# A hybrid trunk step on eight cores: first loads in another order, normalisation steps reordered, the convolution's coefficient blocks built ahead, merge tiles moved into the convolution

## The chip, the cores and the metric

One Trainium2 chip, all 8 of its cores. Each core computes one prompt sequence of 2048 positions and 64 sample rows (16 sequences of 4 positions) with the full weights; the cores do not talk to each other. The metric is the device time in microseconds (us) of the slowest core for one launch.

## What is computed

One layer of a decoder trunk. `xn` is the RMS-normalised input; `pa, pb, pg` are column blocks of one projection.

```python
proj = xn @ w_in                      # 1024 -> 6*1024
a_val, a_gate = split(pa)
glu = a_val * sigmoid(a_gate)
ca  = causal_depthwise_conv(concat(conv_prev, glu), w=(31, 1024)) + b
y_a = silu(layernorm(ca)) @ w_a_out
u, v = split(gelu(pb))
v_n = layernorm(v)                    # mixed over chunks of 128 positions by W_s (8 heads)
y_b = (u * (tril(W_s) @ v_n + b_s)) @ w_b_out
out = (sigmoid(g_a) * y_a + sigmoid(g_b) * y_b) @ w_out
h   = h + out
# channel mixer
a, b = split(rmsnorm(h) @ w_up)       # 1024 -> 2*2816
h   = h + (gelu(causal_depthwise_conv(a, 3)) * b) @ w_down
y   = rmsnorm(h)
```

Outputs are y for prompt and sample, the last rows of the convolutions' inputs, and the normalised v rows of the sample.

## The kernel before

The kernel keeps everything in one SBUF array, `arena`, cut by byte offsets into named views, and one PSUM array of 8 banks that `rbank()` hands out in turn. Helpers (`mm`, `tr`, `act`, `tt`, `tsc`, `stt`, `cp`, `mset`, lines 303 to 337) record one instruction each into the list of its engine, and `Sched` adds the semaphore waits by the bytes touched. So each engine runs its list strictly in the order in which the Python code is written; nothing reorders it. DMAs issued by `S.dma("sp", ...)` stand in SyncE's list, and those of `S.dma("pool", ...)`, which all weight loads use (`load_unit`, 128x1024 f32 in memory, bf16 in SBUF), stand in GpSimd's list between its arithmetic. A DMA also waits for the one before it on its stream (`s_g0` to `s_g23` for SyncE, `s_q0` to `s_q15` for GpSimd).

The stages, in order of the program:

1. **u**: 17 slabs of x (128 rows, the last of 64) are loaded (`xload`), squared and summed on ScalarE (`sq`), scaled on VectorE (`xscale`), turned by 8 TensorE transposes (`xtr`) and copied out as `xnT` (`norm_evac`, VectorE). `xstep` runs these as a software pipeline: step i squares slab i, scales i-1, transposes and copies i-2. `u_mm(c0, w, j)` multiplies w columns by weight block j (8 matmuls) and applies GELU on ScalarE. There are 8 x buffers (`NXB`), and `xscale(c)` also issues `xload(c + 8)` into the buffer that it has read.
2. **v**: for each chunk c `v_mm` (16 matmuls of 512 columns, two GELUs), `v_stats` (two bn_stats, aggregate, add on VectorE, power -0.5 on GpSimd, then a scalar_tensor_tensor that centres), `v_scale` on ScalarE, and `v_mix` (10 matmuls, then two tensor_tensor on VectorE), which runs two chunks behind.
3. **GLU**: two column halves `cb`, each with `s_glu(cb)` for the sample (64 matmuls of 96 columns) and 16 steps p of 16 matmuls with 512 columns, a tanh on ScalarE and one VectorE operation; VectorE also does 8 operations of the sample's convolution in each step (`s_conv`). In the second half `x_trans` transposes groups of channels for the convolution.
4. **convolution**: the depthwise convolution of the prompt is done on TensorE in 16 blocks, `conv(i)`, with 24 matmuls of 128 columns each, against a block of coefficients that `t_build(i)` spreads out from `coef`, in 8 parts: 4 on GpSimd, 3 on ScalarE, 1 on VectorE. Three slots hold such blocks (`tb_t`). Results go to `Y`, whose row q takes 4096 bytes; blocks 0 to 7 write the upper half of each row and blocks 8 to 15 the lower half.
5. **q and merge**: layer norm of Y (`q_stats`, `q_z`), transposes (`q_tr`) and, between them, `run_fill(1)`, which takes one merge tile `half_b(j, ti)` (16 matmuls) from a list of 10; then the rest of the merge.
6. **w_out** with the second RMS norm (`wo_mm`, `n2_scale`, `n2_tr`), **FFN up** (22 blocks of 10 tile halves) and **down** (34 units of 22 matmuls, then the last norm and the store).

## Time and profile before

| | |
|---|---|
| times of three executions | 1183.58, 1340.87 (median), 1375.21 us |
| the profiled execution | 1183.48 us; its slowest core spans 1181.8 us (all cores 1175.4 to 1181.8) |
| TensorE busy | 1088.8 us (92%) |
| VectorE, ScalarE, GpSimd busy | 627.6, 441.2, 186.4 us |
| granted TensorE clock, mean | 0.98 |

The span runs from the first to the last instruction of the slowest core. An engine's busy time counts its compute instructions; "idle before" is the time it stood still just before an instruction, with what released it. The granted clock is 1.00 at 2.4 GHz and 0.5 at 1.2 GHz.

### The profile page before, as it was taken

To read this page: it belongs to the slowest core of one execution; us is meant where nothing else is said; L and a number is where in the kernel's file an instruction comes from. 1 tells how busy PE (TensorE), PEld (TensorE's weight loads), DVE (VectorE), ACT (ScalarE), POOL (GpSimd) and SP (SyncE) were. 2 spreads that over 40 slices of the span, in tenths; PEclk is the share of its full clock that TensorE was granted. 3 is DMA by queue.
4 is the path that set the end of the run, shared out by engine and by line. 5 is a ranking of instruction groups with operands and counts; after the bars stand their busy time and mean duration, and the time that the engine had idled before them with its cause. 6 is when DMAs were issued, how large, how long until landed. Compare 5 with 4: busy or idle time off the path is not lost.

```text
span 1181.8 us, 18831 instructions; the slowest of 8 cores (1175.4 to 1181.8 us)
## 1 busy us (share of the span) xinstructions
PE 1088.8 (92%) x6439; PEld 611.5 (52%) x6527; DVE 627.6 (53%) x1246; ACT 441.2 (37%) x795; POOL 186.4 (16%) x389
## 2 busy tenths in 40 slices
PE   2789986999976999999999999999999999799997
PEld 1546443767664655555554445555555555344443
DVE  1443778565688923333345656666666666223322
ACT  2343433112482731111115555555555555011111
POOL 2323011000175300010001111111111111000000
PEclk9999998999998999999999999999999999899999
DMA  9557201402013032224247742333333322422331
GB/s 241 148 90 118 44 1 18 93 2 41 1 29 55 1 54 37 39 36 82 41 82 248 246 118 45 55 54 55 54 54 55 54 45 43 113 108 107 109 121 73
DMA packets 36140, 88.86 MB, mean 75 GB/s; under 512 B 4112, under 2 KB 6288, under 8 KB 36048
## 3 DMA queue, kind: packets, MB, share of 16 engines
q0 software_dynamic: 21552, 38.75, 20.2%
q1 hardware_dynamic: 14496, 48.92, 12.7%
q8 instruction: 53, 0.87, 0.3%
q14 instruction: 39, 0.32, 0.1%
HBM read 108.05 MB, written 20.04 MB: 108 GB/s over the span
## 4 chain that ended last, share of the span: by engine, by line
PE 80%; DVE 6%; issue 4%; ACT 4%; DMA 4%; POOL 2%; DVEq 0%; SPq 0%; POOLq 0%; ACTq 0%
PE ps L303 78%; ACT arena L314 2%; DMA arena<-w_all 2%; PE ps L306 2%; DVE arena L317 2%; DVE arena L327 2%; DVE arena L575 2%; ACT arena L311 1%; POOL arena L317 1%; DMA arena<-x_p 1%; DVE arena L322 0%; DMA o_vs<-arena 0%; DVE arena L578 0%; DVEq L194 0%; DVE arena L324 0%
## 5 line engine op out<-in xcount | busy, mean ns | idle before, releaser
L303 PE MATMUL ps<-arena 128*128 128x512 bf16 (+7 forms) x5895 | 1060.0, 339 | 63.8 <-DMA arena<-w_all 20.0
L303 PEld LDWEIGHTS ps<-arena 128*128 128x128 bf16 (+1 forms) x5983 | 579.1, 103 | 528.0 <-issue 89.8
L314 ACT ACTIVATE arena<-ps 128x512 f32<-128x512 f32 (+6 forms) x348 | 177.7, 523 | 350.8 <-PE ps L303 263.4
L327 DVE SCALAR_TENSOR_TENSOR arena<-arena 128x64 f32<-128x64 bf16 (+5 forms) x539 | 247.1, 493 | 47.7 <-POOL arena L317 27.1
L314 ACT ACTIVATE arena<-arena 128x512 f32<-128x512 f32 (+4 forms) x192 | 125.9, 676 | 198.1 <-DVE arena L327 178.5
L327 DVE SCALAR_TENSOR_TENSOR arena<-arena,ps 128x512 f32<-128x512 f32 (+4 forms) x120 | 70.0, 589 | 174.4 <-PE ps L303 164.4
L317 DVE TENSOR_TENSOR arena<-arena,ps 128x512 bf16<-128x512 f32 (+2 forms) x143 | 86.4, 614 | 84.9 <-ACT arena L314 84.9
L317 POOL TENSOR_TENSOR arena<-arena 128x1 f32<-128x1 f32 (+1 forms) x85 | 54.6, 647 | 412.6 <-DVE arena L324 290.7
L311 ACT ACTIVATE arena<-arena 128x1024 bf16<-128x1024 f32 (+1 forms) x51 | 53.8, 1054 | 172.4 <-DVE arena L317 149.6
L317 DVE TENSOR_TENSOR arena<-ps,arena 128x1024 bf16<-128x1024 bf16 (+4 forms) x72 | 65.4, 908 | 88.6 <-PE ps L303 86.4
L180 POOL DMA_DIRECT2D arena<-w_all x138 | 74.1, 547 | 195.6 <-PE ps L303 180.0
L314 ACT ACTIVATE arena<-ps,arena 128x512 f32<-128x512 f32 (+3 forms) x150 | 101.2, 705 | 4.1 <-PE ps L306 4.1
L324 DVE TENSOR_SCALAR arena<-arena 128x1 f32<-128x1 f32 (+4 forms) x80 | 23.6, 314 | 109.1 <-ACT arena L311 99.3
L306 PE MATMUL ps<-arena 128*128 128x128 bf16 (+2 forms) x544 | 41.5, 223 | 21.6 <-DVE arena L322 15.1
L334 POOL COPY arena<-arena 128x32 f32<-128x32 f32 (+1 forms) x66 | 13.9, 212 | 260.0 <-ACT arena L314 257.1
L306 PEld LDWEIGHTS ps<-arena 128*128 128x128 bf16 (+2 forms) x544 | 34.4, 100 | 34.3 <-issue 29.3
L327 DVE SCALAR_TENSOR_TENSOR arena<-ps,arena 128x512 f32<-128x512 f32 (+1 forms) x66 | 43.5, 681 | 11.3 <-PE ps L303 11.1
L324 POOL TENSOR_SCALAR arena<-arena 128x384 bf16<-128x384 bf16 x64 | 36.6, 586 | 0.2
L575 DVE BATCH_NORM_STATS2 arena<-arena 128x6 f32<-128x512 f32 (+1 forms) x34 | 23.5, 690 | 18.7 <-ACT arena L314 17.1
L322 DVE TENSOR_SCALAR arena<-arena 128x1 f32<-128x1 f32 (+4 forms) x67 | 29.8, 444 | 3.6
L317 DVE TENSOR_TENSOR arena<-arena 128x512 bf16<-128x512 f32 (+4 forms) x45 | 26.4, 586 | 4.6 <-DVE arena L317 0.2
L337 POOL MEMSET arena<- 128x32 bf16 (+5 forms) x23 | 4.0, 178 | 120.4 <-ACT arena L314 120.4
(19 smaller groups left out, 51.5 us busy)
## 6 DMA issues: line engine op xcount, KB each, us to landing
arena<-w_all POOLq DMA_DIRECT2D x138, 256.0 KB, 5.0
arena<-x_p SPq DMA_DIRECT2D x32, 512.0 KB, 5.1
h1s<-arena SPq DMA_DIRECT2D x16, 512.0 KB, 3.2
arena<-h1s SPq DMA_DIRECT2D x16, 512.0 KB, 3.9
o_yp<-arena SPq DMA_DIRECT2D x16, 512.0 KB, 2.9
o_ch<-st_a SPq DMA_DIRECT2D x1, 1664.0 KB, 18.7
arena<-dw_t POOLq DMA_DIRECT2D x4, 384.0 KB, 4.5
arena<-st_a POOLq DMA_DIRECT2D x1, 960.0 KB, 18.5
```

The lines of the kernel that those rows point to most:

```text
L180: e.items.append(("op", lambda q, o=out, i=in_: q.dma_start(out=o, in_=i), stream, 16))
L303: S.op("pe", lambda q: q.matmul(out, lhsT=lhsT, rhs=rhs, start=start, stop=stop), [out], [lhsT, rhs], inc=stop)
L306: S.op("pe", lambda q: q.transpose(out=out, in_=in_, identity=ident), [out], [in_, ident], inc=inc)
L311: S.op("act", lambda q: q.activation(out=out, in_=in_, func=func, scale=scale, bias=bias, accum_out=accum), [out, accum], ins)
L314: S.op("act", lambda q: q.activation(out=out, in_=in_, func=func, scale=scale, bias=bias), [out], ins)
L317: S.op(en, lambda q: q.tensor_tensor(out=out, in0=in0, in1=in1, op=op), [out], [in0, in1])
L322: S.op(en, lambda q: q.tensor_scalar(out=out, in0=in0, scalar1=s1, scalar2=None, op0=op0), [out], ins)
L324: S.op(en, lambda q: q.tensor_scalar(out=out, in0=in0, scalar1=s1, scalar2=s2, op0=op0, op1=op1), [out], ins)
L327: S.op("dve", lambda q: q.scalar_tensor_tensor(out=out, in0=in0, scalar=scalar, in1=in1, op0=op0, op1=op1), [out], [in0, in1] + ([scalar] ...
L334: S.op(en, lambda q: q.tensor_copy(out=out, in_=in_), [out], [in_])
L337: S.op("pool", lambda q: q.memset(out, v), [out], [])
L575: S.op("dve", lambda q, i=i, a=a: q.bn_stats(out=s[:cs, 6 * i:6 * i + 6], in_=a), [s[:cs, 6 * i:6 * i + 6]], [a])
```

## The change

- **u stage.** Four x slabs instead of eight are issued at once, with two weight blocks beside them; weight blocks 2 and 3 and then 4 to 7 are issued from GpSimd between the first four normalisations. The slabs 4 to 7 are issued after that, each behind the landing of a weight block. A first GELU on one column is issued before any data. The first eight groups of 128 columns are computed in tiles of 256 columns, and a table `at` says after which tile which `xstep` comes.
- **v stage.** The centring is taken out of `v_stats` as `v_center` and put behind the mix of the chunk two before. The last scale and mixes are interleaved with `s_glu(1)`, which is cut in two parts.
- **Convolution.** `t_build` takes a string of engines for its 8 parts and has another layout; six slots instead of three, the three new ones in the lower halves of rows of Y, so that blocks 0, 1, 3, 4 and 5 are built on GpSimd in the second GLU half, block 2 after it, and 6 to 15 in the convolution. Four weight blocks of the merge are loaded in the convolution (at block 5), and four merge tiles run in it (after blocks 9, 11, 13 and 15); the list has 15 tiles. The state for the sample's convolution is loaded ahead of the GLU weights. `q_stats` adds and takes the power for four rows in one instruction.
- **w_out.** The transposes run two chunks behind instead of one, with three buffers.
- **Down.** The first four units run their first 20 matmuls before any runs the last two. The last chunk is normalised and stored in two halves.

```diff
+        for c in range(1, 4):
             xload(c)
+        mset(nh, -0.5)
+        act(stat[0][:, 31:32], nh, AF.Gelu)
...
+        for c in range(4):
+            sq(c)
+            if c:
+                norm_evac(c - 1, 34)
+            if 0 < c < 3:
+                u_load()
+            xscale(c)
+            xtr(c)
+            if c == 2:
+                u_mm(0, 256, 0)
+            if c == 3:
+                u_mm(0, 256, 1)
         u_load()
+        norm_evac(3, 34)
+        nready[0] = 4
+        for c in range(4, 8):
+            xload(c, after=[wtok[min(c - 2, len(wtok) - 1)]])
+            if len(uW) < 8:
+                u_load()
+        work = [(0, 256, j) for j in (2, 3)] + [(256, 256, j) for j in range(4)]
+        work += [(c0, 256, j) for j in range(4, 8) for c0 in (0, 256)]
+        work += [(c0, 256, j) for c0 in (512, 768) for j in range(8)]
+        work += [(c0, w, j) for c0, w in TILES[2:] for j in range(8)]
+        at = {2: 4, 5: 5, 8: 6, 11: 7, 15: 8, 18: 9, 21: 10, 24: 11, 27: 12, 29: 13, 31: 14, 33: 15, 35: 16, 37: 17, 39: 18}
         for n, (c0, w, j) in enumerate(work):
+            while nready[0] < -(-(c0 + w) // 128) and nready[0] < 17:
+                xstep()
             u_mm(c0, w, j)
+            if n in at and nstep[0] <= at[n]:
+                xstep()
...
-            if i < len(order):
-                v_stats(order[i])
+            v_stats(order[i])
             if i >= 2:
                 v_mix(order[i - 2])
+            v_center(order[i])
...
+        tslots = [tslot(R1, 2048), tslot(R1 + 6144, 2048), tslot(R2, 2048),
+                  tslot(OFF_D + 4 * 4096, 4096), tslot(OFF_D + 12 * 4096, 4096), tslot(OFF_D + 7 * 4096, 16384)]
+        tb_of = lambda i: tslots[i] if i < 6 else tslots[i % 3]
...
+        v_scale(order[16])
+        s_glu(1, (0,))
+        v_mix(order[15])
         for cb in (1, 0):
-            s_glu(cb)
+            if cb == 1:
+                s_glu(1, (1,))
+                v_mix(order[16])
+            else:
+                s_glu(0)
...
-                    if p in (2, 4):
-                        coef_load((p - 2) // 2)
-                    if p in (10, 12):
-                        t_build((p - 10) // 2)
+                    if p in (0, 1):
+                        coef_load(p)
+                    if p in (3, 5, 8, 10, 13):
+                        t_build({3: 0, 5: 1, 8: 3, 10: 4, 13: 5}[p], "pppppppp")
...
+        t_build(2, "daadaapp")
+        for i in range(16):
+            if i + 8 < 16:
+                x_trans(i + 8)
+            conv(i)
+            if i < 3:
+                t_build(i + 6, "pppppaaa")
+            elif 6 <= i < 13:
+                t_build(i + 3, "ppppaaaa")
+            if i in (1, 2):
+                coef_load(i + 1)
...
+            if i == 5:
+                mload(4)
...
+            if i in (9, 11, 13, 15):
+                run_fill(1)
...
-            if i >= 1:
-                n2_tr(i - 1)
+            if i >= 2:
+                n2_tr(i - 2)
             n2_scale(i)
...
+        early = [(i, q, rbank()) for i in range(2) for q in range(2)]
+        for i, q, b in early:
+            dn_mm(i, q, b, range(20))
+        for i, q, b in early:
+            dn_mm(i, q, b, range(20, NFF))
+            dn_add(i, q, b)
```

SyncE's list at the start of the program, before. `x_p` is the input x, a row is one slab, `x7` means seven such rows, `s_act` and `s_dve` are ScalarE's and VectorE's counters.

```order
L180 DMA arena<-x_p 128x1024
L180 DMA arena<-col_a 128x288
L180 DMA arena<-x_p 128x1024 x7
L180 DMA arena<-x_p 128x1024 [waits s_g0,s_act,s_dve]
L180 DMA arena<-x_p 128x1024 [waits s_dve] x7
```

The same place after the change.

```order
L180 DMA arena<-x_p 128x1024
L180 DMA arena<-col_a 128x288
L180 DMA arena<-x_p 128x1024 x3
L180 DMA arena<-x_p 128x1024 [waits s_g0,s_act,s_dve]
L180 DMA arena<-x_p 128x1024 [waits s_g2,s_act,s_dve]
L180 DMA arena<-x_p 128x1024 [waits s_g3,s_act,s_dve]
L180 DMA arena<-x_p 128x1024 [waits s_g4,s_act,s_dve]
L180 DMA arena<-x_p 128x1024 [waits s_q2]
L180 DMA arena<-x_p 128x1024 [waits s_q3]
L180 DMA arena<-x_p 128x1024 [waits s_q4]
L180 DMA arena<-x_p 128x1024 [waits s_q5]
```

The slabs 8 to 11, issued by `xscale(0)` to `xscale(3)` in the new first loop (the rows that wait for `s_g0`, `s_g2`, `s_g3`, `s_g4`), now stand ahead of the slabs 4 to 7, which wait for the landing of the weight blocks 2 to 5 (`s_q2` to `s_q5`).

VectorE's list in the v stage, one chunk of 16 alike, before.

```order
L575 BN_STATS arena<-arena 128x6 [waits s_act]
L575 BN_STATS arena<-arena 128x6 [waits s_act,s_dve]
L578 BN_AGGR arena<-arena 128x2 [waits s_dve]
L322 TENSOR_SCALAR arena<-arena 128x1 [waits s_dve]
L327 SCALAR_TENSOR_TENSOR arena<-arena 128x1024 [waits s_pool]
L317 TENSOR_TENSOR arena<-arena,ps 128x4x128 [waits s_pe] x2
```

The same place after the change.

```order
L588 BN_STATS arena<-arena 128x6 [waits s_act]
L588 BN_STATS arena<-arena 128x6 [waits s_act,s_dve]
L591 BN_AGGR arena<-arena 128x2 [waits s_dve]
L322 TENSOR_SCALAR arena<-arena 128x1 [waits s_dve]
L317 TENSOR_TENSOR arena<-arena,ps 128x4x128 [waits s_pe] x2
L327 SCALAR_TENSOR_TENSOR arena<-arena 128x1024 [waits s_pool]
```

The centring, which waits for GpSimd's power, and the two products of the mix have changed places.

GpSimd's list in the convolution after the change, from its part of block 6 to its part of block 9. The 128x3x128 rows are parts of `t_build`, the MEMSETs belong to `x_trans` and wait for its copy on ScalarE, `dw_t` is the source of `coef`.

```order
L324 TENSOR_SCALAR arena<-arena 128x3x128 [waits s_pool,s_pe]
L324 TENSOR_SCALAR arena<-arena 128x3x128 x4
L337 MEMSET arena 128x8x4 [waits s_act]
L324 TENSOR_SCALAR arena<-arena 128x3x128 [waits s_pool,s_pe]
L324 TENSOR_SCALAR arena<-arena 128x3x128 x4
L180 DMA arena<-dw_t 128x1536 [waits s_pool,s_dve]
L337 MEMSET arena 128x8x4 [waits s_act]
L324 TENSOR_SCALAR arena<-arena 128x3x128 [waits s_q5,s_pe]
L324 TENSOR_SCALAR arena<-arena 128x3x128 x4
L180 DMA arena<-dw_t 128x1536 [waits s_pool]
L337 MEMSET arena 128x8x4 [waits s_act] x3
L180 DMA arena<-w_all 128x1024 x4
```

Before, the third coefficient load stood four blocks ahead of its first reader; now its first reader (the row that waits for `s_q5`) is the next arithmetic behind it.

## Rows read from the trace of the kernel before

**Rows 1.** Busy time by stretch, whole core; the second line names the columns.

```profile
core 2 of [0, 1, 2, 3, 4, 5, 6, 7], span 1181.8 us
core 2: us, PE busy (x) PEld busy (x) DVE busy (x) ACT busy (x) POOL busy (x), PEclk, DMA share, GB/s
0.00:115.60 115.60, 81.67 (x542) 51.14 (x548) 39.85 (x65) 41.96 (x85) 36.37 (x62) 0.96 0.68 149
115.60:211.60 96.00, 79.52 (x480) 40.38 (x489) 71.41 (x121) 36.28 (x51) 10.26 (x18) 0.93 0.19 33
211.60:329.20 117.60, 116.17 (x628) 79.47 (x640) 73.60 (x290) 30.97 (x49) 6.77 (x17) 1.00 0.14 27
329.20:373.30 44.10, 28.39 (x456) 26.22 (x458) 40.47 (x67) 30.34 (x53) 36.70 (x73) 0.98 0.19 30
373.30:414.80 41.50, 39.05 (x293) 23.60 (x296) 32.45 (x77) 24.49 (x38) 12.52 (x20) 0.94 0.19 31
414.80:618.80 204.00, 203.12 (x1187) 112.92 (x1201) 67.32 (x121) 41.85 (x84) 17.49 (x33) 1.00 0.30 52
```

**Rows 2.** DMA queues of the page: packets, MB, share of 16 engines.

```profile
q0 software_dynamic: 21552, 38.75, 20.2%
q1 hardware_dynamic: 14496, 48.92, 12.7%
```

**Rows 3.** Timeline, u stage: start, length, instruction, idle before and its releaser.

```profile
10.49 1.06 ACT L311 ACTIVATE arena<-arena 128x1024 bf16<-128x1024 f32 x1 [2.52 <-DMA arena<-x_p]
...
14.58 0.58 POOL L180 DMA_DIRECT2D arena<-w_all  x1
...
23.66 1.87 PE L303 MATMUL ps<-arena 128*128 128x256 bf16 x8 [4.07 <-DMA arena<-w_all]
...
55.28 5.32 PE L303 MATMUL ps<-arena 128*128 128x512 bf16 x12 [4.10 <-DVE arena L317]
...
61.73 3.62 PE L303 MATMUL ps<-arena 128*128 128x512 bf16 x16
65.19 0.61 PE L306 MATMUL ps<-arena 128*128 128x128 bf16 x8
```

**Rows 4.** Timeline, end of the v stage, VectorE and TensorE.

```profile
192.24 1.28 DVE L327 SCALAR_TENSOR_TENSOR arena<-arena 128x1024 f32<-128x1024 f32 x1 [0.80 <-POOL arena L317]
...
194.64 1.48 DVE L575 BATCH_NORM_STATS2 arena<-arena 128x6 f32<-128x512 f32 x2
...
199.89 1.49 DVE L575 BATCH_NORM_STATS2 arena<-arena 128x6 f32<-128x512 f32 x2
...
205.42 10.75 PE L303 MATMUL ps<-arena 128*128 128x128 bf16 x93 [3.39 <-ACT arena L314]
```

**Rows 5.** Timeline, second GLU half, VectorE without and with GpSimd building.

```profile
299.34 1.65 DVE L327 SCALAR_TENSOR_TENSOR arena<-arena 128x64 f32<-128x64 bf16 x8
...
314.07 1.90 DVE L327 SCALAR_TENSOR_TENSOR arena<-arena 128x64 f32<-128x64 bf16 x8
```

**Rows 6.** Groups by form, 330 to 374 us: busy us, mean ns, idle before.

```profile
L324 POOL TENSOR_SCALAR arena<-arena 128x384 bf16<-128x384 bf16 x56 | 31.7, 581 | 0.2
L303 PE MATMUL ps<-arena 128*128 128x128 bf16 x384 | 24.0, 219 | 9.6 <-ACT arena L314 4.5 <-DVE arena L322 3.1 <-DVE arena L327 1.6
```

**Rows 7.** Timeline, first merge tiles, TensorE.

```profile
373.30 12.79 PE L303 MATMUL ps<-arena 128*128 128x512 bf16 x47 [6.14 <-DMA arena<-w_all]
```

**Rows 8.** DMA issues of the page: count, KB each, us to landing.

```profile
arena<-dw_t POOLq DMA_DIRECT2D x4, 384.0 KB, 4.5
```

**Rows 9.** Waits of TensorE, 615 to 702 us: us in total, times, longest.

```profile
PE ps L306 <- ACT arena L314: 4.6, 9, 0.8
```

**Rows 10.** Timeline, start of the down stage, TensorE.

```profile
1011.97 0.61 PE L303 MATMUL ps<-arena 128*64 128x512 bf16 x1 [5.81 <-DMA arena<-w_all]
1014.27 7.96 PE L303 MATMUL ps<-arena 128*64 128x512 bf16 x23 [1.70 <-DMA arena<-w_all]
```

**Rows 11.** Timeline, the last chunk.

```profile
1175.17 1.06 ACT L311 ACTIVATE arena<-arena 128x1024 bf16<-128x1024 f32 x1 [8.35 <-DVE arena L317]
```

More of the change, by code:

```diff
@@ L413, in build_program @@
         S.dma("sp", colA, col_a)
-        for c in range(1, NXB):
+        for c in range(1, 4):
             xload(c)
+        mset(nh, -0.5)
+        act(stat[0][:, 31:32], nh, AF.Gelu)
         mset(ident_f, 0.0)
@@ L619, in build_program @@
         order = [16] + list(range(16))
-        for i in range(len(order) + 2):
-            if i < len(order):
-                v_mm(order[i])
-            if 1 <= i <= len(order):
+        for i in range(len(order)):
+            v_mm(order[i])
+            if i >= 1:
                 v_scale(order[i - 1])
-            if i < len(order):
-                v_stats(order[i])
+            v_stats(order[i])
             if i >= 2:
                 v_mix(order[i - 2])
+            v_center(order[i])
         sg = [view(R2 + 2048 * i, F32, (128, 512)) for i in range(3)]
@@ L671, in build_program, with s_glu @@
         s_conv = []
-        def s_glu(cb):
-            for jp in range(2):
+        def s_glu(cb, parts=(0, 1)):
+            for jp in parts:
                 b = rbank()
@@ L688, in s_glu @@
                 cp("dve", glub[:, j0:j0 + 2, 480:544], gluS[:, j0:j0 + 2, 32:96])
-            for k in range(CW):
+            for k in range(CW) if 1 in parts else ():
                 for j in range(cb * 4, cb * 4 + 4):
@@ L696, in s_glu @@
                                                            yS[:, j, :], ALU.mult, ALU.add))
-            if cb == 0:
+            if cb == 0 and 1 in parts:
                 S.dma("sp", o_ca, gluS)
@@ L792, in mload, with run_fill @@
                 key = morder[mnext[0]]
-                wtile[key] = load_unit(mkind[key], RING[mnext[0] % 6])
+                wtile[key] = load_unit(mkind[key], OFF_C + 25344 + 2048 * mnext[0] if mnext[0] < 4 else RING[(mnext[0] - 4) % 6])
                 mnext[0] += 1
-        mload(6)
         scount = [0]
+        late = [False]
+        fill = [(j, ti) for j in range(3) for ti in range(5)]
+        def run_fill(n):
+            for _ in range(n):
+                if fill:
+                    half_b(*fill.pop(0))
         xqn = lambda a, nn: a.rearrange("p (q n) -> p n q", n=nn)
@@ L916, in build_program @@
         h1 = [view(OFF_C + 12288 + 4096 * i, F32, (128, D)) for i in range(3)]
-        xs2 = [view(OFF_D + 2048 * i, BF16, (128, D)) for i in range(2)]
+        xs2 = [view(OFF_D + 2048 * i, BF16, (128, D)) for i in range(3)]
+        UPR = [RING[i] for i in (2, 3, 0, 1, 4, 5)]
         upW = {}
```

215 lines of the change are left out of this document (115 added, 100 removed).

## The prediction

> **What bounds the kernel now.** I read the table by stretch first [rows 1], to see where TensorE (PE) isn't working. Between 414.8 and 618.8 us it is busy 203.12 of 204.00 us at a granted clock of 1.00, and in the GLU stage 116.17 of 117.60: nothing is to be had there. The losses lie where dependence chains or loads set the pace. The u stage takes 115.6 us with 81.67 busy and a clock of 0.96, the v stage 96.0 with 79.52 busy at 0.93, the convolution 44.1 with 28.39 busy. The stretch behind it has 39.05 of 41.5 busy, but at 0.94. So the idle time is one loss and the half clock behind it is another: after 4.10 us of idle, 12 matmuls of 512 columns take 5.32 us (443 ns each), against 3.46 us for 16 a little later (65.19 less 61.73, 216 ns each) [rows 3]. The clock was at its lower level, 1.2 GHz, for those 12. I then read, stretch by stretch, which wait ends last.
>
> **The u stage.** At 10.49 us the second slab of x has landed, but weight block 1 is issued only at 14.58, behind GpSimd's powers and behind eight slabs in the DMA engines, and TensorE has waited 4.07 us for it when it starts at 23.66 [rows 3]. One transfer is priced by the queues: q0 moved 38.75 MB in 20.2% of 1181.8 us, so 0.262 MB of a weight block is 1.6 us of all engines; a 0.524 MB slab on q1 is 12.7% × 1181.8 / 48.92 × 0.524 = 1.6 us too [rows 2]. After the change block 1 is issued at about 3 us and blocks 2 and 3 from about 13.5, (slab 1's landing, 1.25 us of square, the power and the issue), so the first tiles of 256 columns run from about 18 us on. Against this stands SyncE's new order: slabs 8 to 11 go ahead of 4 to 7, though they are needed last. By 20 us some 11 transfers are through; four slabs and four weight blocks alternate, slab 4 lands at about 28 to 29 and slab 7 near 36. `sq(4)` stands in ScalarE's list from tile n=2 on and holds up the GELUs behind it. Slab 5 lands near 32; its square, the VectorE steps behind it and the transposes of slab 4 (which stand behind tile n=8) put those at about 34.4, and the copy of slab 5, on which tile n=14 waits, ends near 41.5. Before, the same point (first 512 columns done, next ones ready) is 55.28. From it to 115.6 is 60.3 us; the idle at its start is left out of that already, and the 12 slow matmuls cost 12 × (443 − 216) = 2.7 us, so 57.6 remain. This would end the stage at 99.1. I add 1.5 for a half clock after the waits at n=9 and n=14: 100.6. **Saving 15 us.** Bounds: 0 (slabs 4 to 7 land as late as the stage can bear, and the warm-up is paid twice), and 22 (they don't bind).
>
> **The v stage.** VectorE sets the pace: from one chunk's bn_stats to the next is 199.89 − 194.64 = 5.25 us, of which 0.80 is idle before the centring, waiting for the power on GpSimd [rows 4]. With the mix's products in this gap the period is 4.45. The products are ready: their matmuls stand behind `v_mm` of the same step, as the second GELU does. TensorE's own work per chunk is 16 + 2 matmuls of 512 columns at 216 ns and 8 of a quarter of that, 4.3 us, just under it. 15 steady steps × 0.80 = 12.0. At the end TensorE waits 3.39 us for the last scale [rows 4], then does the last mix and `s_glu(1)` behind a cold start. With the two halves of `s_glu(1)` in the gap I take 4. **Saving 16 us.** Bounds: 8 (TensorE's 4.3 is 4.6 in truth, and half of the end) and 17. The GpSimd list now has the sample's state load in front of 16 weight loads, and the last of those waits for its stream; v's first power is behind them. That may cost 0 to 4 of this, and I take none, as the loads are issued some 18 us ahead.
>
> **GLU.** TensorE sets it, nothing gained. GpSimd gets 40 parts of `t_build` here instead of 8. With 4 parts beside it, a group of 8 VectorE operations of `s_conv` takes 1.90 us instead of 1.65 [rows 5], so 40 parts add 10 × 0.25 = 2.5 us to an engine that is busy 73.60 of 117.6 [rows 1]. Cost 0; if that cover were gone, 2.5.
> The Trainium skill (SBUF — State Buffer, Who interferes with whom) says that a VectorE instruction with two SBUF inputs and a GpSimd instruction that reads SBUF exclude each other for a whole instruction. By that, 40 builds at 581 ns would put 23 us on VectorE here, and the stage would end some 7 us later; rows 5 show a quarter of a microsecond for four.
>
> **Convolution and q.** Before, TensorE is idle 9.6 us in it, waiting for ScalarE's and VectorE's parts, then 6.14 for the first merge weights, and 12 cold matmuls open the merge (47 in 12.79 us) [rows 6, 7]. Now four merge tiles (three of 16 × 216 ns and one of 288 columns, 1.95 us: 12.3) go into it and blocks 0 to 5 are ready. But GpSimd becomes the pace. It has 15 parts for blocks 6 to 8 and 28 for 9 to 15, 43 × 0.581 = 25.0 us [rows 6]; the part of block 8 waits for a coefficient load just issued, 4.5 us [rows 8], with ScalarE's part of it and the copies of `x_trans` behind it; four weight loads cost 4 × 0.58 more to issue (the row of 14.58 us in [rows 3]). On a time line from the stage's start: block 6 can begin on GpSimd at about 5.3, when ScalarE has done its parts of block 2 and the first copy of `x_trans`; blocks 6 and 7 take 5 × 0.581 each and end at 11.2; the issue of the load (0.6) and its 4.5 us give 16.3, block 8's five parts 19.2, the second coefficient load and the four weight loads 22.0, block 9's four parts 24.4. TensorE then has 7 blocks of 24 × 58 ns = 1.4 us and 12.3 us of tiles left, and ends at about 46.5 against 44.1 before, with the four tiles done. Later blocks need 2.3 us each on GpSimd, less than a block and half a tile on TensorE, 3.1. That gains 12.3 − 2.4 = 9.9; the cold start of the merge (12 × 0.22 = 2.6) goes too, and the batched power about 0.5. **Saving 13 us.** Bounds: 3 (GpSimd's parts at a stride cost a third more, 8 us, and a wait behind them) and 18.
>
> **w_out.** 9 waits for ScalarE's scale, 4.6 us in all [rows 9]; with transposes two chunks behind, the scale has 3.9 us more. **Saving 4.6**, bounds 3 and 5.
>
> **Down.** TensorE waits 5.81 and 1.70 us for the last two weight blocks, which can be issued only when the last FFN block has been read; then 23 matmuls take 7.96 us instead of 5.0 [rows 10]. The new order puts 60 more matmuls (13 us) in front of the first that needs them. 5.81 + 1.70 + 3.0 + 0.4 = **10.9 us**, bounds 8 and 11.
>
> **Tail.** The last square (1.06 us [rows 11]) covers half a row, and half the store goes out early: **0.6**, bounds 0 and 1.2.
>
> **Sum.** 15 + 16 + 0 + 13 + 4.6 + 10.9 + 0.6 = 60.1. The profiled execution took 1183.48 us (span 1181.8 and 1.7 around it), so 1183.5 − 60.1 = **1123.4 us**. That execution equals the fastest of the three shown (1183.58). Their median, 1340.87, is of executions that took longer than the trace explains; the forecast is for executions like the traced one.
>
> **The rivals.**
> *The front gains nothing.* The four slabs in the wrong order cost what the earlier weights give: 1123.4 + 15 = 1138. For it: the order itself. Against: TensorE has the nine tiles n=0 to 8 to do meanwhile, about 8 us of work at the upper clock.
> *GpSimd is too slow in the convolution.* Its end moves by 10: 1133 to 1136. For it: 25.0 us of parts in one list with two dependent loads; against: its 581 ns has held beside VectorE.
> *Exclusion in GLU.* GpSimd's 40 parts hold up VectorE for whole instructions; the stretch has 117.6 − 73.6 = 44 us of slack in 32 steps [rows 1], so 1.4 in each of the 12 steps that the builds lie in; 23 less 16 is 7: 1130. For it: that more of GpSimd's work now lies there than ever before. Against it: [rows 5].
> *The change doesn't do what it says in v*: TensorE's 4.3 us is really 4.9, the gap closes by half: 1123.4 + 8 = 1131.
> *Slower than before.* A denser TensorE is granted less clock. The work that TensorE sets is about 1070 us, so 1% of clock is 10.7 us and the gain is gone from 5.6% on. The two longer executions are 13 to 16% above the third; at 1340.87/1183.58 the forecast would be 1273. Against it: the densest stretch (203.12 of 204.00 us busy) has a clock of 1.00 [rows 1], and the low clock in [rows 3] stands behind idle time.
>
> **How the numbers follow.** Forecast as summed, 1108 to 1132: 0.50. Front nothing: 0.15. GpSimd in the convolution: 0.12. Exclusion 0.05, v half 0.10; two of these together, 1145 to 1155: 0.05. Clock: 0.03. Below 1108 nothing is expected but the upper bounds together (22 + 17 + 18 + 5 + 11 + 1 = 74, 1109). The range reaches over the single rivals: 1107 to 1146. About 2% (24 us) is what a measurement can tell from no change; faster than that means under 1160, which all cases but the clock and a worse pile-up meet: faster 0.93, same 0.04, slower 0.03.
>
> **What would show it.** The v stage starts near 100 us; x slab 4 is used at about 29, after slab 8 has landed; TensorE idles before the transposes of slab 4 and at tile n=14. The bn_stats in v come every 4.4 to 4.6 us. In GLU no wait of TensorE for VectorE. In the convolution TensorE waits about 7 us in blocks 5 and 9, released through `dw_t`, and GpSimd is busy without a break behind it. No wait of TensorE for weights at the start of down or merge, and the clock stays 1.00 there. Wrong would be a v period of 5 us or more, a v start beyond 110, or a granted clock below 1.00 in stretches without idle time.

## The result

The changed kernel takes **1146.88 us** (median of four executions, 1145.76 to 1147.83), against 1183.6 us for the kernel before: ratio 0.9689, 95% interval 0.9665 to 0.9712. Some executions, of the kernel before and of some of the variants below, run 2 to 16% longer at a lower granted clock; every figure here leaves them out. The change is faster by 36.7 us, where 60.1 were forecast; 1146.88 lies just above the range. Direction and most terms were right; 23.4 us are missing.

The profile after is of an execution of 1147.06 us. First, from the page's head, busy time by engine.

```profile
PE 1085.1 (95%) x6591; PEld 619.2 (54%) x6591; DVE 619.0 (54%) x1222; ACT 440.1 (38%) x799; POOL 191.6 (17%) x398
```

TensorE has as much to do as before (1085.1 against 1088.8 us); what went is idle time. Then the busy time by stretch, with the columns of [rows 1], cut at the ends of the stages: u, v, GLU, the first part of the convolution, and, behind merge and w_out, feed-forward with the start of down.

```profile
0.00:110.50 110.50, 76.56 (x594) 55.88 (x594) 39.44 (x64) 41.60 (x91) 35.56 (x63) 0.95 0.66 144
110.50:200.30 89.80, 82.90 (x516) 42.30 (x515) 71.44 (x124) 39.68 (x54) 9.90 (x18) 0.95 0.33 55
200.30:316.50 116.20, 115.54 (x632) 78.34 (x630) 78.08 (x286) 27.56 (x42) 25.47 (x48) 1.00 0.11 23
316.50:367.00 50.50, 42.01 (x529) 35.22 (x530) 33.93 (x58) 31.95 (x56) 32.81 (x66) 0.90 0.34 54
...
659.20:1010.00 350.80, 348.50 (x1923) 188.10 (x1921) 222.91 (x391) 182.22 (x362) 49.81 (x136) 1.00 0.35 63
```

The u stage still has 34 us without TensorE work and a clock of 0.95. The first part of the convolution has 8.5 us of idle time and a clock of 0.90. GLU is full, and so is the feed-forward stage but for 2.3 us.

Stages don't end at a common instant, so I compare the two executions between the same instructions. The first such mark is the first bn_stats of the v stage. VectorE's timeline has it, first before, then after:

```profile
114.51 0.69 DVE L575 BATCH_NORM_STATS2 arena<-arena 64x6 f32<-64x512 f32 x1 [15.66 <-ACT arena L314]
```
```profile
113.31 0.69 DVE L588 BATCH_NORM_STATS2 arena<-arena 64x6 f32<-64x512 f32 x1 [15.66 <-ACT arena L314]
```

| from mark to mark | before, us | after, us | saved | forecast |
|---|---|---|---|---|
| start to first bn_stats of v | 114.5 | 113.3 | 1.2 | 15 |
| to the bn_stats of the third chunk | 12.1 | 15.5 | −3.4 | 0 |
| 14 steady steps of v | 73.3 | 61.75 | 11.5 | 12 |
| end of v to the first tanh of GLU | 13.6 | 9.7 | 3.8 | 4 |
| GLU to the transposes of yS | 115.8 | 116.2 | −0.5 | 0 |
| convolution, q, merge | 290.3 | 279.6 | 10.7 | 13 |
| w_out | 67.3 | 63.1 | 4.2 | 4.6 |
| feed-forward | 315.3 | 318.0 | −2.7 | 0 |
| down to the last sum | 172.3 | 161.2 | 11.0 | 10.9 |
| tail | | | 0.4 | 0.6 |

The saved column adds up to 36.2, against 36.7 timed. Four lines carry the miss: the start (13.8 us too much), two waits that I hadn't seen (3.4 and 2.7), and 2.3 in the convolution. The first tile of v comes near 110.5 us, just beyond the 110 that the prediction named as a sign of being wrong.

**Where the u stage stops.** TensorE's timeline of the u stage after the change (start, length, instruction, idle before and its releaser):

```profile
24.50 1.01 PE L306 MATMUL ps<-arena 128*128 128x128 bf16 x8 [3.71 <-DVE arena L322]
...
42.70 1.01 PE L306 MATMUL ps<-arena 128*128 128x128 bf16 x8 [6.01 <-DVE arena L322]
43.50 4.72 PE L303 MATMUL ps<-arena 128*128 128x256 bf16 x24
...
51.98 1.91 PE L303 MATMUL ps<-arena 128*128 128x256 bf16 x16 [1.57 <-DVE arena L317]
...
54.17 2.78 PE L303 MATMUL ps<-arena 128*128 128x256 bf16 x24
```

No weight block is waited for any more, as one was in [rows 3]. But the transposes of slab 4 at 42.70 come after 6.01 us of idle, and the 24 matmuls behind them take 4.72 us where 24 like them take 2.78 at 54.17: 197 and 116 ns each, the lower and the upper clock. The chain of waits says what was late:

```profile
23.60 0.76 DVE arena L322
24.43 0.33 SPq L180
24.86 13.65 DMA arena<-x_p
```

Slab 4 is issued at 24.86, behind `xscale(3)` and slab 11's issue at 24.43, and lands 13.65 us later. And why `xscale(3)` is so late shows on ScalarE's and GpSimd's timelines:

```profile
20.88 0.38 ACT L314 ACTIVATE arena<-ps 128x256 bf16<-128x256 f32 x1 [5.53 <-PE ps L303]
21.16 1.05 ACT L311 ACTIVATE arena<-arena 128x1024 bf16<-128x1024 f32 x1
...
23.24 2.28 POOL L180 DMA_DIRECT2D arena<-w_all  x4
```

ScalarE stood 5.53 us before the GELU of the first tile, with the square of slab 3 in its list behind it. So the square ran at 21.16, GpSimd issued the weight blocks 4 to 7 at 23.24 behind its power, and SyncE the slabs 11 and 4 to 7 from 24.43. Meanwhile the DMA engines ran at less than half (windows of 3 us, columns as above; the window from 18 to 21 us has 0.99):

```profile
21.00:24.00 3.00, 0.00 (x0) 0.00 (x0) 1.60 (x3) 1.30 (x3) 1.29 (x3) 1.00 0.41 152
24.00:27.00 3.00, 2.50 (x16) 2.05 (x17) 1.57 (x2) 0.00 (x0) 1.52 (x3) 1.00 0.38 44
```

**The second chunk of v.** ScalarE and TensorE, after:

```profile
128.12 1.09 ACT L314 ACTIVATE arena<-ps 128x512 f32<-128x512 f32 x2 [8.43 <-DMA o_vs<-arena]
...
130.38 1.86 PE L303 MATMUL ps<-arena 128*128 128x128 bf16 x10 [4.79 <-ACT arena L314]
```

The sample's rows for `o_vs` are written back into `vt[1]` and stored from there. The store takes 6.90 us, and the third chunk's GELU wants `vt[1]`. When it is issued, eight of the 16 weight blocks are still on their way (DMA share 1.06 to 1.10 here), since the sample's state now goes ahead of them. Before, three were left, the store took 3.49 us, and the same wait of TensorE was 1.38 us.

**The convolution.** After, GpSimd, ScalarE and TensorE at the third load of coefficients:

```profile
327.44 0.59 POOL L180 DMA_DIRECT2D arena<-dw_t  x1
...
333.61 2.82 POOL L324 TENSOR_SCALAR arena<-arena 128x384 bf16<-128x384 bf16 x5 [5.44 <-DMA arena<-dw_t]
...
333.81 1.62 ACT L314 ACTIVATE arena<-arena 128x384 bf16<-128x384 bf16 x3 [7.47 <-DMA arena<-dw_t]
...
336.49 1.44 PE L303 MATMUL ps<-arena 128*128 128x128 bf16 x12 [8.06 <-ACT arena L314]
337.73 1.06 PE L306 MATMUL ps<-arena 128*128 128x128 bf16 x8
338.58 2.66 PE L303 MATMUL ps<-arena 128*128 128x128 bf16 x24
```

One wait of 8.06 us where I had put about 7 in blocks 5 and 9 together. Behind it TensorE runs at the lower clock (granted 0.50 from 336 to 341 us): the three rows take 1.44, 1.06 and 2.66 us, where the same work took 0.83, 0.61 and 1.50 shortly before, 2.2 us more. GpSimd's next wait, at 341.42 us, is 0.44 for TensorE, not the other way round.

**The start of the feed-forward stage.**

```profile
660.14 0.78 SPq L180 DMA_DIRECT2D arena<-col_f  x1
...
665.89 0.78 ACT L314 ACTIVATE arena<-ps,arena 128x512 f32<-128x512 f32 x1 [1.56 <-DMA arena<-col_f]
...
671.83 4.40 PE L303 MATMUL ps<-arena 128*128 128x288 bf16 x21 [2.30 <-DVE arena L317]
```

The four factors per channel are loaded only here, and the first scaled copy waits for them; TensorE waits for a bank about 5 us later. Before, the load stood at the same place: issued at 687.75, landed at 691.62, first used at 691.84. It had 0.2 us to spare. Now it takes 5.67 us to land instead of 3.87; why it takes longer is not shown.

### The profile page after: what moved, and what is told of

Same layout as the page of the kernel before. It is cut to its first block, busy times and chain, and to the rows that moved or that the text cites. A ratio compares the mean times of both kernels' runs of the same rounds, so it can differ in the third digit from the quotient of the medians.

```text
span 1145.5 us, 19024 instructions; the slowest of 8 cores (1140.0 to 1145.5 us)
## 1 busy us (share of the span) xinstructions
PE 1085.1 (95%) x6591; PEld 619.2 (54%) x6591; DVE 619.0 (54%) x1222; ACT 440.1 (38%) x799; POOL 191.6 (17%) x398
## 4 chain that ended last, share of the span: by engine, by line
PE 86%; DVE 4%; DMA 4%; issue 3%; ACT 2%; POOL 0%; DVEq 0%; SPq 0%; ACTq 0%; POOLq 0%
PE ps L303 84%; PE ps L306 2%; DMA arena<-x_p 2%; DVE arena L327 1%; ACT arena L314 1%; DVE arena L317 1%; ACT arena L311 1%; DVE arena L588 1%; DMA o_vs<-arena 1%; DMA arena<-dw_t 1%; DMA arena<-col_f 0%; POOL arena L324 0%; DVE arena L322 0%; SPq L180 0%; DVE arena L591 0%
## 5 line engine op out<-in xcount | busy, mean ns | idle before, releaser
L303 PE MATMUL ps<-arena 128*128 128x512 bf16 (+5 forms) x6047 | 1058.2, 337 | 25.4 <-ACT arena L314 15.2
L303 PEld LDWEIGHTS ps<-arena 128*128 128x128 bf16 (+1 forms) x6047 | 585.6, 103 | 480.3 <-issue 39.6
L314 ACT ACTIVATE arena<-ps 128x224 f32<-128x224 f32 (+7 forms) x356 | 179.8, 516 | 350.6 <-PE ps L303 269.1
L327 DVE SCALAR_TENSOR_TENSOR arena<-arena 128x64 f32<-128x64 bf16 (+5 forms) x540 | 251.9, 501 | 39.8 <-POOL arena L317 15.3
L314 ACT ACTIVATE arena<-arena 128x512 f32<-128x512 f32 (+4 forms) x186 | 121.8, 673 | 169.8 <-DVE arena L327 141.6
L311 ACT ACTIVATE arena<-arena 128x1024 bf16<-128x1024 f32 (+2 forms) x52 | 54.0, 1039 | 167.1 <-DVE arena L317 137.8
L317 POOL TENSOR_TENSOR arena<-arena 128x1 f32<-128x1 f32 (+2 forms) x73 | 47.1, 646 | 380.4 <-DVE arena L324 275.5
L324 DVE TENSOR_SCALAR arena<-arena 128x1 f32<-128x1 f32 (+4 forms) x81 | 23.7, 312 | 102.5 <-ACT arena L311 97.4
L324 POOL TENSOR_SCALAR arena<-arena 128x384 bf16<-128x384 bf16 x85 | 49.6, 602 | 7.0 <-DMA arena<-dw_t 5.4
L588 DVE BATCH_NORM_STATS2 arena<-arena 128x6 f32<-128x512 f32 (+1 forms) x34 | 23.4, 689 | 22.4 <-ACT arena L314 20.9
L780 DVE BATCH_NORM_STATS2 arena<-arena 128x6 f32<-128x512 f32 (+1 forms) x34 | 21.4, 678 | 0.1
```

What stands on the lines that cost most here:

```text
L303: S.op("pe", lambda q: q.matmul(out, lhsT=lhsT, rhs=rhs, start=start, stop=stop), [out], [lhsT, rhs], inc=stop)
L311: S.op("act", lambda q: q.activation(out=out, in_=in_, func=func, scale=scale, bias=bias, accum_out=accum), [out, accum], ins)
L314: S.op("act", lambda q: q.activation(out=out, in_=in_, func=func, scale=scale, bias=bias), [out], ins)
L317: S.op(en, lambda q: q.tensor_tensor(out=out, in0=in0, in1=in1, op=op), [out], [in0, in1])
L324: S.op(en, lambda q: q.tensor_scalar(out=out, in0=in0, scalar1=s1, scalar2=s2, op0=op0, op1=op1), [out], ins)
L327: S.op("dve", lambda q: q.scalar_tensor_tensor(out=out, in0=in0, scalar=scalar, in1=in1, op0=op0, op1=op1), [out], [in0, in1] + ([scalar] ...
```

## The experiments

Every kernel is the changed one (1146.88) with the edit shown. Each figure is the median of its executions, the range behind it is that of the same executions, and each ratio is against the kernel before on the same chip (1183.5 to 1183.6 us).

### What the new front is worth, and why

`front_old`: the loads, `xstep` and the `work` list of before in place of the new ones.

```diff
-        for c in range(4):
-            sq(c)
...
-        work = [(0, 256, j) for j in (2, 3)] + [(256, 256, j) for j in range(4)]
+        xready(1)
+        u_load()
+        xready(2)
+        u_load()
+        for js in ((0, 1, 2, 3), (4, 5, 6, 7)):
+            for c0 in (0, 256):
+                work += [(c0, 256, j) for j in js]
```

> The changed kernel with the u stage's loads, steps and order of tiles of the kernel before; all else is as changed. By my forecast the new front is worth 15 us, so this would take 1162. By the comparison of the two traces the first bn_stats of the v stage comes at 113.3 us in the changed kernel against 114.5 before, so the new front is worth 1 us: 1147 to 1149. If the new front costs something later (the transfer of o_vs, which takes 6.9 us beside the weight loads where it took 3.5), it is worth less than nothing: 1144 to 1147.

Measured: 1145.33 us (1143.72 to 1146.37), ratio 0.9676 (0.9662 to 0.9690). The old front is as fast as the new one, or 1.6 us faster; the ranges touch. The 15 us of the forecast aren't there. Its first bn_stats of v comes at 114.04 us, against 113.31. Its store of `o_vs` takes 7.55 us and TensorE waits 5.45 for it, so that wait comes with the old front too and isn't the new one's doing.

`x_order`: slabs 8 to 11 behind 4 to 7.

```diff
-            if c + NXB < 17:
+            if 4 <= c and c + NXB < 17:
                 xload(c + NXB)
...
+        for c in range(8, 12):
+            xload(c)
         work = [(0, 256, j) for j in (2, 3)] + [(256, 256, j) for j in range(4)]
```

> The changed kernel with one difference: slabs 8 to 11 of x are no longer asked for inside xscale, ahead of slabs 4 to 7, but behind them. Theory A (order of the loads): slab 4 is late because four slabs that are needed last go ahead of it and because its issue at 24.9 us stands behind xscale(3). Then slab 4 is issued near 18 us and lands by about 26 instead of 38.5, the wait of TensorE before its transposes (6.01 us at 42.7) goes, and the kernel takes 1140 to 1143 us, 4 to 7 less than the changed kernel's 1146.9. Theory B (amount of the loads): what paces the u stage is the sum of bytes that must be in by then, in any order, and weight blocks 4 to 7 are as late as before; slab 4 lands before 30, but the wait moves to later slabs or weights, and the time is 1146 to 1148.

Measured: 1139.37 us (1138.94 to 1139.96), ratio 0.9627 (0.9613 to 0.9642), 7.5 less. Theory A holds, and a little more than its bound. TensorE's timeline of this kernel, and SyncE's issue of slab 4:

```profile
35.96 0.61 PE L306 MATMUL ps<-arena 128*128 128x128 bf16 x8
36.40 2.78 PE L303 MATMUL ps<-arena 128*128 128x256 bf16 x24
...
17.06 0.33 SPq L180 DMA_DIRECT2D arena<-x_p  x1
```

The wait of 6.01 us before the transposes of slab 4 is gone, and so is the half clock behind it (24 matmuls in 2.78 us). Slab 4 is issued at 17.06, when weight block 2 has landed (16.98), near the 18 expected, and lands at 22.92; slab 5 follows at 20.24, when block 3 has landed. The first bn_stats of v comes at 105.61 instead of 113.31.

`x_order_sq3`: the first tile also behind the square of slab 3.

```diff
             xscale(c)
+            if c == 3:
+                u_mm(0, 256, 0)
             xtr(c)
-            if c == 2:
-                u_mm(0, 256, 0)
```

> As x_order, and the first tile of the u stage, u_mm(0, 256, 0), is written behind the square of slab 3, so that this square no longer stands behind that tile's GELU on ScalarE. TensorE's order is the same. Theory A: the square of slab 3 starts up to 1.5 us earlier, weight blocks 4 to 7 are issued by GpSimd that much earlier, and the DMA engines' hole at 21 to 27 us (0.38 to 0.41 busy) shrinks: 1 to 2 us less than x_order, 1138 to 1142. Theory B: equal to x_order within 1 us.

Measured: 1137.55 us (1136.88 to 1138.01), ratio 0.9610 (0.9594 to 0.9626), 1.8 less than `x_order`. The transposes of slab 3, which wait for its scale:

```profile
21.16 0.73 PE L306 MATMUL ps<-arena 128*128 128x128 bf16 x8 [0.43 <-DVE arena L322]
```

They come at 21.16 instead of 24.08 in `x_order`, with 0.43 us of wait instead of 3.71. The one GELU in ScalarE's list had cost 2.9 us at this place, of which 1.8 reached the end (the first bn_stats of v comes at 103.81, against 105.61), since 3.06 us of wait now stand before slab 4 again.

### The store of o_vs

`ovs_buf`:

```diff
-                stt(vt[c % 3][:cs], vt[c % 3][:cs], vstat[c][:cs, 15:16], lnbb, ALU.mult, ALU.add)
-                S.dma("sp", o_vs, vt[c % 3][:cs])
+                stt(vso, vt[c % 3][:cs], vstat[c][:cs, 15:16], lnbb, ALU.mult, ALU.add)
+                S.dma("sp", o_vs, vso)
```

> The changed kernel, but the sample's v rows for the output o_vs are written to a buffer of their own instead of back into vt[1], which the third chunk of the v stage needs. Theory A (a held buffer): ScalarE's 8.43 us and TensorE's 4.79 us of idle near 130 us come from the transfer out of vt[1], 6.90 us long beside 17 loads; with the own buffer they go and the kernel takes 1142 to 1144 us, 3 to 5 less. Theory B (the loads themselves, or VectorE, set the pace there): the wait only changes its name, 1146 to 1147.5.

Measured: 1143.31 us (1142.90 to 1143.84), ratio 0.9660 (0.9646 to 0.9675), 3.6 less. TensorE of this kernel runs without a break from the u stage far into v:

```profile
95.25 76.75 PE L303 MATMUL ps<-arena 128*128 128x288 bf16 x472
```

Theory A holds: it was a held buffer, not the loads as such, which are all still there. The store itself still takes 7.12 us; nothing waits for it.

### The convolution

`coef_early`: the third load of coefficients ahead.

```diff
         t_build(2, "daadaapp")
+        coef_load(2)
...
-            if i in (1, 2):
-                coef_load(i + 1)
+            if i == 2:
+                coef_load(3)
```

> The changed kernel, but the third load of coefficients, coef_load(2), is issued right behind the builds of block 2, ahead of those of block 6, instead of behind those of block 7, so some 5 to 6 us earlier. Theory A: TensorE's stall of 8.06 us at 336 us (released by ScalarE, whose parts of block 8 wait 7.47 us for dw_t, with a copy of x_trans queued behind them) is this load's landing, 5.4 us, taken late; it goes nearly whole: 1139 to 1142 us, 5 to 8 less than the changed kernel's 1146.9. Theory B: GpSimd paces the convolution. Its list now waits at the load's issue until ScalarE has read the old coefficients, blocks 6 and 7 come later, and the stall is only divided among blocks 6 to 9: 1144 to 1147.

Measured: 1138.92 us (1138.15 to 1139.51), ratio 0.9622 (0.9608 to 0.9637), 8.0 less. The wait of 8.06 us is gone, and the lower clock behind it. TensorE's waits in the convolution of this kernel, from block 0 to the first merge tile, are these (a row of 0.70 before the transposes of yS left out):

```profile
325.54 0.83 PE L303 MATMUL ps<-arena 128*128 128x128 bf16 x12 [0.40 <-ACT arena L314]
328.11 0.83 PE L303 MATMUL ps<-arena 128*128 128x128 bf16 x12 [0.62 <-ACT arena L314]
335.06 1.50 PE L303 MATMUL ps<-arena 128*128 128x128 bf16 x24 [1.21 <-ACT arena L314]
337.90 29.39 PE L303 MATMUL ps<-arena 128*128 128x512 bf16 x256 [1.34 <-DMA arena<-w_all]
```

Theory B, that GpSimd paces the convolution and the stall would only be divided, falls, and with it the rival "GpSimd is too slow": 3.6 us of waits in four places are left, and none is released by GpSimd's arithmetic. That the gain equals the stall is in part chance: 8.06 and 2.2 went, and 3.2 of smaller waits are new.

`no_fill`: the four merge tiles behind the convolution.

```diff
-            if i in (9, 11, 13, 15):
-                run_fill(1)
         late[0] = True
+        run_fill(4)
```

> The changed kernel, but the four merge tiles that lie between blocks 9 to 15 of the convolution stand behind it. They are 12.3 us of TensorE's work. Theory A: most of them lie in time in which GpSimd builds blocks 9 to 15 (2.4 us a block against 1.4 us of TensorE), so without them TensorE waits there about 7 us and starts the merge at the half clock (up to 2.6 us): 1153 to 1157. Theory B: the builds ahead in late-written rows have already taken the waits away, and the tiles are only moved: 1146 to 1149. Theory C: everything in the convolution is set by GpSimd and the fill is wholly free: 1159.

Measured: 1151.93 us (1151.62 to 1153.22), ratio 0.9735 (0.9719 to 0.9751), 5.1 more. The time lies between theories A and B: putting the 12.3 us of tiles into the convolution is worth 5.1. How much of that is waits filled and how much is a merge that starts at the upper clock is not shown, since its trace isn't used.

### The order of v and of down

`v_old`:

```diff
+            v_center(order[i])
             if i >= 2:
                 v_mix(order[i - 2])
-            v_center(order[i])
```

> The changed kernel, but in the v stage the centring stands in front of the mix's two products on VectorE again, as before. By my forecast the order is worth 0.80 us in each of the steady steps, 11.5 by the comparison of the traces (period 5.23 against 4.41 us over 14 chunks): 1158 to 1159 us. If the shorter period came from elsewhere in the change (the halves of s_glu(1), the sample's state load moved ahead), less than 8 of it comes back: below 1155.

Measured: 1157.62 us (1156.60 to 1158.89), ratio 0.9781 (0.9767 to 0.9796), 10.7 more. VectorE, first of this kernel, then of the changed one:

```profile
159.80 1.48 DVE L588 BATCH_NORM_STATS2 arena<-arena 128x6 f32<-128x512 f32 x2
...
162.65 1.28 DVE L327 SCALAR_TENSOR_TENSOR arena<-arena 128x1024 f32<-128x1024 f32 x1 [0.80 <-POOL arena L317]
...
165.04 1.48 DVE L588 BATCH_NORM_STATS2 arena<-arena 128x6 f32<-128x512 f32 x2
```
```profile
146.39 1.48 DVE L588 BATCH_NORM_STATS2 arena<-arena 128x6 f32<-128x512 f32 x2
...
149.59 1.28 DVE L327 SCALAR_TENSOR_TENSOR arena<-arena 128x1024 f32<-128x1024 f32 x1
150.79 1.48 DVE L588 BATCH_NORM_STATS2 arena<-arena 128x6 f32<-128x512 f32 x2
```

The wait of 0.80 is back, and with it the period of 5.24; without it the period is 4.40.

`down_old`:

```diff
-            dn_mm(i, q, b, range(20))
-        for i, q, b in early:
-            dn_mm(i, q, b, range(20, NFF))
+            dn_mm(i, q, b, range(NFF))
```

> The changed kernel, but in the down stage each chunk runs over all 22 weight blocks in one piece, as before, so that the first sum wants the last two blocks at once. By my forecast the order is worth 10.9 us and by the comparison of the traces 11.0: 1157 to 1158. If the steps that merged or moved elsewhere (two transposes moved into the first feed-forward tiles, the ring's order) had given it, 1147 to 1150.

Measured: 1156.67 us (1154.77 to 1158.04), ratio 0.9770 (0.9753 to 0.9788), 9.8 more. The waits of [rows 10] stand there again, a little longer than in the kernel before:

```profile
988.16 0.60 PE L303 MATMUL ps<-arena 128*64 128x512 bf16 x1 [6.58 <-DMA arena<-w_all]
990.75 49.60 PE L303 MATMUL ps<-arena 128*64 128x512 bf16 x222 [1.98 <-DMA arena<-w_all]
```

### The factors of the feed-forward convolution

`colf_early`:

```diff
+        S.dma("sp", colF.rearrange("p a b -> p (a b)"), col_f.rearrange("p a b -> p (a b)"))
         for i in range(3):
             xr_load(i)
```

The same line is taken out ahead of the feed-forward loop.

> The changed kernel, but the load of colF (the four factors of the feed-forward convolution) is issued ahead of the w_out stage instead of behind it, where it stands on SyncE's queue behind a load that waits for a buffer. Theory A: it is what TensorE's new wait of 2.30 us at 671.8 us comes from (issued 660.1, landed 665.8, the first scaled copy out of the bank waits for it); without it the first feed-forward tiles gain 2 to 3 us with the half clock behind the wait: 1144 to 1145. Theory B: the table load on ScalarE and the last norm steps would make TensorE wait there anyway: 1146 to 1147.

Measured: 1143.35 us (1142.91 to 1145.73), ratio 0.9664 (0.9650 to 0.9679), 3.5 less. Theory A, and somewhat more than it said. In its trace TensorE waits 1.09 us at this place instead of 2.30, and the granted clock from 670 to 676 us is 1.00 instead of 0.72.

### Together

`best_five` has the five edits that helped.

> The changed kernel with five edits at once: slabs 8 to 11 of x behind 4 to 7, the first tile behind the square of slab 3, the buffer of its own for o_vs, coef_load(2) behind the builds of block 2, and colF's load ahead of w_out. Alone they gave 7.3, 2.1, 3.6, 8.0 and 3.5 us. Theory A: they lie at five separate places of TensorE's path and add up, 24.5 us: 1121 to 1125. Theory B: an earlier place only feeds a later wait (an earlier end of the u stage puts the loads of st_a and the value weights nearer to their use), and 18 us or less stays: above 1128.

Measured: 1124.19 us (1124.12 to 1124.35), ratio 0.9501 (0.9486 to 0.9516): 22.7 less, of the 24.4 that the five gave one by one. They add up almost whole, as theory A has it.

`best_steps` adds the list of the u stage.

```diff
-        at = {2: 4, 5: 5, 8: 6, 11: 7, 15: 8, 18: 9, 21: 10, 24: 11, 27: 12, 29: 13, 31: 14, 33: 15, 35: 16, 37: 17, 39: 18}
+        at = {2: 4, 5: 5, 7: 6, 9: 7, 13: 8, 16: 9, 19: 10, 22: 11, 24: 12, 26: 13, 28: 14, 31: 15, 33: 16, 36: 17, 39: 18}
...
-            if n == 32:
+            if n == 30:
+                setup_w()
+            if n == 34:
                 setup_v()
```

`setup_w` is the first line of `setup_v`, the product that makes WsT.

> As best_five, and in the u stage the steps that make slabs 6 to 13 ready stand one or two tiles earlier in the list, and the product that setup_v's matmuls wait for stands four tiles ahead of them. Theory A: the waits of TensorE for VectorE that the u stage still has (1.57, 0.53, 0.44, 2.72 and 2.94 us, 8.2 together) are distances in the list, and most go, with the half clock behind the two of near 3 us: 4 to 8 us less than best_five. Theory B: the slabs themselves land too late for the earlier steps, and the waits move to them: within 2 us of best_five.

Measured: 1115.16 us (1114.34 to 1116.66), ratio 0.9427 (0.9410 to 0.9443), 9.0 less than `best_five`. Whole waits of TensorE up to 110.5 us (total, times, longest), first of the changed kernel, then of this one:

```profile
PE ps L306 <- DVE arena L322: 26.2, 6, 9.1
PE ps L303 <- DVE arena L317: 7.7, 4, 2.9
```
```profile
PE ps L306 <- DVE arena L322: 18.1, 6, 9.0
PE ps L306 <- DVE arena L324: 2.1, 1, 2.1
```

The four waits for VectorE's copies are gone; in `best_five` they were 8.1 us. The steps and `setup_v` were moved together, so what each gave is not shown.

`best_nogate` drops the wait of slabs 4 to 7 for the weight blocks.

```diff
-            xload(c, after=[wtok[min(c - 2, len(wtok) - 1)]])
+            xload(c)
```

> As best_steps, but slabs 4 to 7 of x are asked for at once, each not behind the landing of a weight block. Theory A: the gates keep weight blocks 2 and 3 in front; without them these land later, the first tiles wait, and it takes 1 to 4 us more than best_steps. Theory B: the gates only hold back slabs while the DMA engines have a hole at 21 to 27 us, and it takes 1 to 3 us less.

Measured: 1114.08 us (1112.30 to 1114.63), ratio 0.9412 (0.9395 to 0.9429), 1.1 less than `best_steps`; the ranges overlap, so which of the two orders is better stays open. Both mechanisms are in its trace: TensorE waits 1.77 and 0.61 us for weight blocks, which the gates prevent, and the first bn_stats of v comes at 93.40, against 95.17.

```profile
25.41 6.27 PE L303 MATMUL ps<-arena 128*128 128x256 bf16 x56 [1.77 <-DMA arena<-w_all]
```

This is the fastest kernel measured here: 69.4 us less than before, 32.8 less than the changed one.

## Why the prediction was right, and where it failed

**u stage: 15 forecast, 1.2 measured. The step that failed is the date of slab 4.** "By 20 us some 11 transfers are through" and "slab 4 lands at about 28 to 29": it landed at 38.5. The prediction had the wrong order in view, but took slabs 4 to 7 as issued by 20 us and the DMA engines as busy throughout. They were issued from 24.86, because slab 11's issue stood ahead of them on SyncE's queue, this waits for `xscale(3)`, that for the square of slab 3, and that stood behind a GELU which waited for TensorE. The DMA engines ran at 0.41 and 0.38 meanwhile. With the order mended the issue is at 17.06 and the landing at 22.92 (`x_order`). Tile n=14, which I had at 41.5, came at 51.98: 10.5 us. The other 3.3 us are a second step, "57.6 remain": I took the rest of the stage over from before. There it holds one wait of 3.53 us; now it holds four (0.52, 0.44, 2.72 and 2.93, together 6.6), because the table `at` puts a step right in front of the tile that needs it, and `setup_v`'s matmuls right behind their product. 15 − 10.5 − 3.3 = 1.2. Both are shown: 7.5 and 1.8 us came back when just the slabs' order and the square's place were mended, and 9.0 with the steps and `setup_v`.

The Trainium skill (DMA: Bandwidth & Descriptors, Anatomy of one DMA — SWDGE (gpsimd) path) says that the DMA engines don't wait on semaphores, and that any such wait happens on the issuing sequencer before dispatch. By that rule, the trace agrees: slab 4 is issued 0.43 us behind slab 11 (24.43 and 24.86), though its own condition is the landing of weight block 2, which `x_order` has at 16.98.

**v stage: 16 forecast, 15.3 measured.** The period of 4.45 came out as 4.41, and `v_old` gives back 10.7 of the 11.5. The end of v gave 3.8 for 4. The rival that TensorE's 4.3 us are 4.9 is refuted. But the prediction looked only at the steady step: it named the state load ahead of the weight loads and took none of its 0 to 4 us, and looked for its effect at GpSimd's power. It struck at the store of `o_vs`, which holds `vt[1]`, 3.4 us; with it the stage gave 11.9 in all. That the store is slow because of the state load is read from the traces; no run puts that load back.

**GLU: 0 forecast, −0.5 measured.** GpSimd's 40 builds cost VectorE more than I had said, and nobody waited for it. The groups by form of the GLU stage (busy, mean ns), before and then after:

```profile
L327 DVE SCALAR_TENSOR_TENSOR arena<-arena 128x64 f32<-128x64 bf16 x238 | 49.8, 279 | 0.0
```
```profile
L327 DVE SCALAR_TENSOR_TENSOR arena<-arena 128x64 f32<-128x64 bf16 x236 | 54.1, 300 | 0.0
```

21 ns more on each of 236 is 5.0 us, against 2.5 by [rows 5]. Nearly all of it lies in 20 of these products. The others take 271 to 287 ns, with a build beside them or not; the 20 take 517 to 611 ns, and each of them ends 69 to 74 ns behind the end of one of GpSimd's builds. Two of them, each with its build:

```profile
290.72 0.59 POOL L324 TENSOR_SCALAR arena<-arena 128x384 bf16<-128x384 bf16 x1
290.77 0.61 DVE L327 SCALAR_TENSOR_TENSOR arena<-arena 128x64 f32<-128x64 bf16 x1
...
291.29 0.66 POOL L324 TENSOR_SCALAR arena<-arena 128x384 bf16<-128x384 bf16 x1
291.50 0.52 DVE L327 SCALAR_TENSOR_TENSOR arena<-arena 128x64 f32<-128x64 bf16 x1
```

So a product can be held until the build is over. The one just ahead of it, which starts as the build begins, still goes through, and then the build is the longer one: 0.66 us, where undisturbed ones take 0.58. The products with one operand in PSUM (128x512) keep their 686 to 690 ns beside a build.
By the rule of the Trainium skill (SBUF — State Buffer, Who interferes with whom), a VectorE instruction with two SBUF inputs and a GpSimd instruction that reads SBUF exclude each other for a whole instruction; the trace agrees. What is refuted is the amount in the rival of exclusion, 23 us on VectorE and 7 on the stage: it took each of the 40 builds as lost whole, but only 20 products were held, for about a quarter of a microsecond each, and VectorE had time to spare.

**Convolution: 13 forecast, 10.7 measured.** The mechanism was right (one load of coefficients, with ScalarE's parts and the copies of `x_trans` behind it), though the load took 5.94 us to land, not 4.5. Wrong was the term for GpSimd's pace: I let TensorE wait there about 7 us in two places for GpSimd's sake. It waited 8.06 in one, and it was the load's landing, 5.44 us seen from GpSimd and 7.47 from ScalarE; `coef_early` removed that wait. Missing was a term for the lower clock behind such a wait, 2.2 us. The two together are more than the 2.3 that are missing, so something else in this sum came out better than forecast; what, is not shown.

**w_out 4.2 for 4.6, down 11.0 for 10.9, tail 0.4 for 0.6**: right by their own steps; `down_old` bears out the largest at 9.8.

**Feed-forward: nothing forecast, −2.7 measured.** A step that was missing. I had looked for what the shorter w_out takes away and not at the load behind its end, which had 0.2 us to spare before and landed 1.8 us later against its issue after. `colf_early` gives 3.5 back.

Of the rivals, "the front gains nothing" at 1138 came true, and with the two unseen waits (6.1) and the convolution's 2.3 that makes 1146.4, near the measured 1146.88. The clock was no cause: 1.00 in every stretch without idle time.

## What to carry to other kernels

Follow a load back to its issue, and along the list of the queue that issues it: here one activation in ScalarE's list held back a square, a power, four weight loads and five slabs, and left the DMA engines at 0.4 for 6 us in the stage that waits for data. When a stage is made tighter, look at what its first and last instructions meet (a buffer still being stored, a small load issued only just before it is read): three such edits of one or two lines gave 15.1 us, and together with the order of the first loads and the steps they nearly doubled what the large change had brought (36.7 us, then 69.4). Take the end of a stage from an instruction, not from the edge of a window.

## What the runs showed of the hardware

- TensorE's clock after idle time: behind 6.01 us without work, 24 matmuls of 256 columns took 4.72 us (197 ns each; granted clock 0.55 from 42 to 48 us, so mostly at the lower level, 1.2 GHz), and 2.78 us (116 ns each, granted clock 1.00, 2.4 GHz) where the wait was taken away (`x_order`). So the 6.01 us cost nearly 8.
- A store of 64 rows took 6.90 us to complete with eight weight blocks of the same core on their way, where it had taken 3.49 with three. The load of `dw_t` took 4.50 to 11.64 us (median of four 6.6), against 4.5 before [rows 8].
- GpSimd's builds and VectorE's small products (two operands in SBUF) kept each other out: 20 of 238 products took 517 to 611 ns instead of about 279 and ended 69 to 74 ns behind the end of a build. On average that is 8% (279 to 300 ns); single groups of eight took up to 2.48 us, where [rows 5] have 1.65 and 1.90. Products with one operand in PSUM were not lengthened.
